# Gate products of the second and third block divided in column blocks and placed between the units of the attentions

## What is computed

```python
# second block: h is the block's input after its first layer norm, 256 x 1024
proj = h @ w_in                                   # 2208 columns: c_q 384, c_kv 256, k_rope 32, q_d, k_d, v_d
q  = rms_norm(c_q)  @ w_q_b                       # 8 heads of 96, MLA
kv = rms_norm(c_kv) @ w_kv_b                      # 8 heads of 64 + 64
o_mla, o_diff = causal attention of q, kv; differential attention of q_d, k_d, v_d with a bias by distance
gates = sigmoid(h @ w_gate + b_gate)              # 2048 columns
mix = (gates[:, :1024] * (o_mla @ w_up_mla) + gates[:, 1024:] * (o_diff @ w_up_diff)) @ w_o
# third block: u is the normed input
qa, ka, va, qb, kb, vb, qi, ki, wi, g = split(u @ w_in)   # 5444 columns, g the last 2048
out_a = attention of qa, ka, va over the 64 best keys by the index scores of qi, ki, wi (DSA)
out_b = causal attention of qb, kb, vb (MoBA, whose one block holds all 256 keys here)
gates = sigmoid(g + b_gate)
h = h + (gates[:, :1024] * (out_a @ w_branch_dsa) + gates[:, 1024:] * (out_b @ w_branch_moba)) @ w_out
```

## Time and profile before

| | |
|---|---|
| time, median of 3 | 2945.77 us |
| profiled execution | 2943.41 us, span 2941.8 us |
| TensorE busy with matmuls | 2766.5 us, 94% |
| VectorE busy | 2075.8 us, 71% |
| ScalarE busy | 1623.6 us, 55% |
| mean granted TensorE clock | 0.957 of full speed |

### The profile page before, as it was taken

One profiled execution on the slowest core, in us unless ns is written; L12 is line 12 of the kernel. 1 busy time (PEld: TensorE's weight loads), 2 busy tenths in 40 slices (PEclk: granted clock), 3 DMA queues, 4 the chain that ended last, 5 costly groups with the idle time before them and its releaser, 6 DMA issues.

```text
span 2941.8 us, 38545 instructions
## 1 busy us (share of the span) xinstructions
PE 2766.5 (94%) x12256; PEld 2192.8 (75%) x12256; DVE 2075.8 (71%) x2462; ACT 1623.6 (55%) x2026; POOL 208.1 (7%) x212
## 2 busy tenths in 40 slices
PE   8997999999999999999799897799997999988999
PEld 5665888888888888888588785677786887876787
DVE  4556999999999999999744664665546445775544
ACT  2323888888888888888544334343443443343443
POOL 0001111111111111111100000000000000100000
PEclk9997999999999999999799997799998999977999
DMA  8755999999999999999755561253554555622564
GB/s 319 233 173 204 357 355 354 355 353 354 358 354 352 355 355 354 355 350 349 255 165 178 168 193 43 82 200 112 170 187 151 178 178 177 185 71 92 169 185 139
DMA packets 263618, 700.16 MB, mean 238 GB/s; under 512 B 29656, under 2 KB 128384, under 8 KB 213824
## 3 DMA queue, kind: packets, MB, share of 16 engines
q1 hardware_dynamic: 249780, 685.13, 66.3%
q0 software_dynamic: 9648, 8.42, 0.9%
q10 hardware_dynamic: 4124, 5.77, 0.6%
HBM read 706.51 MB, written 24.15 MB: 248 GB/s over the span
## 4 chain that ended last, share of the span: by engine, by line
PE 86%; DVE 7%; issue 2%; ACT 2%; DMA 2%; SPq 1%; POOL 0%; DVEq 0%; ACTq 0%; POOLq 0%
PE bank L571 23%; PE bank L572 23%; PE bank L573 23%; PE bank L1025 3%; PE bank L1027 3%; PE bank L1026 3%; PE bank L731 2%; PE bank L689 1%; DMA raw<-in_w_in 1%; PE bank L911 1%; PE bank L707 1%; PE bank L881 1%; PE bank L937 1%; PE bank L637 1%; DVE w_lo L1150 1%
## 5 line engine op out<-in xcount | busy, mean ns | idle before, releaser
L571 PE MATMUL bank<-w_hi,HTh 128*128 128x512 f32 x2964 | 1193.8, 403 | 37.8 <-DVE HTl L1199 33.1
L572 PE MATMUL bank<-w_lo,HTh 128*128 128x512 f32 x2964 | 1177.4, 397 | 0.0
L573 PE MATMUL bank<-w_hi,HTl 128*128 128x512 f32 x2964 | 1177.2, 397 | 0.0
L2058 ACT ACTIVATE w_hi<-raw 128x1024 fp32r<-128x1024 f32 x444 | 461.5, 1054 | 545.8 <-PE bank L573 379.6
L1150 DVE TENSOR_TENSOR w_lo<-raw,w_hi 128x1024 fp32r<-128x1024 f32 x444 | 528.4, 1215 | 309.9 <-ACT w_hi L2058 305.8
L571 PEld LDWEIGHTS bank<-w_hi,HTh 128*128 128x128 f32 x2964 | 563.1, 190 | 179.9 <-DVE HTl L1199 36.9
L573 PEld LDWEIGHTS bank<-w_hi,HTl 128*128 128x128 f32 x2964 | 562.7, 190 | 133.5
L572 PEld LDWEIGHTS bank<-w_lo,HTh 128*128 128x128 f32 x2964 | 563.4, 190 | 123.2
L1773 DVE TENSOR_TENSOR w_lo<-arena,w_hi 128x1024 fp32r<-128x1024 f32 x256 | 315.9, 1234 | 45.5 <-ACT w_hi L2247 45.5
L1773 DVE TENSOR_TENSOR w_lo<-raw,w_hi 128x1024 fp32r<-128x1024 f32 x256 | 298.8, 1218 | 3.4 <-ACT w_hi L2292 2.0
L2247 ACT ACTIVATE w_hi<-raw 128x1024 fp32r<-128x1024 f32 x252 | 266.8, 1059 | 59.2 <-PE bank L573 59.2
(11 more groups left out here) (304 smaller groups left out, 2256.1 us busy)
## 6 DMA issues: line engine op xcount, KB each, us to landing
raw<-in_moe_w SPq DMA_DIRECT2D x128, 1024.0 KB, 4.9
arena<-in_moe_w SPq DMA_DIRECT2D x128, 1024.0 KB, 4.9
raw<-in_ffn_w SPq DMA_DIRECT2D x264, 256.0 KB, 3.4
H<-in_moe_w SPq DMA_DIRECT2D x64, 1024.0 KB, 4.9
MIX<-in_moe_w SPq DMA_DIRECT2D x64, 1024.0 KB, 4.9
raw<-in_ffn_w_gu SPq DMA_DIRECT2D x176, 256.0 KB, 3.4
raw<-in_w_in SPq DMA_DIRECT2D x80, 512.0 KB, 4.7
raw<-in_ffn_w_down SPq DMA_DIRECT2D x88, 256.0 KB, 3.4
```

Of the source, the lines that this page charges most:

```text
L571: pe.matmul(acc, xh, wh, start=start, stop=False)
L572: pe.matmul(acc, xh, wl, start=False, stop=False)
L573: return pe.matmul(acc, xl, wh, start=False, stop=stop)
L2058: act.activation(w_hi[:, n % PARTS, 0:m], raw[:, n % RAW, 0:m], ACT.Copy).then_inc(hi_done, 1)
```

## The change

The gate product of the second block is divided in three: its first 512 columns (`gate2_0`) stand before `q_b`, the next 512 (`gate2_1`) between `kv_b` and the turning of the queries, the last 1024 (`gate2_fill`, 2 blocks) inside the attentions, one block in `A_MLA` and one in `A_DIFF`. The third block's `in3` loses its last 2048 columns; they become `gate3`, 4 blocks, two in `A_MOBA` and two in `A_DSA`. Inside an attention TensorE runs a quantum (`part_of_product`: one 128-deep step for both token tiles, 6 matmuls of 128x512) in each of the first 8 steps, one per step in the second block, two in the third. The blocks use banks 2 and 3 alone, so the scores use 0 and 1. VectorE splits and reads out between the units (`gates_between`, `gates3_between`, `fill_out`), ScalarE makes the high parts there (`highs_between`).

Since `HTh`/`HTl` now have to keep the block's input rows until the end of `A_DIFF`, the latent rows are split into `CTh`/`CTl`, which lie over the bias table and `AFTl`; the bias table of `A_DIFF` is therefore loaded after `kv_b` and not at the end of the first block. The two sigmoids are taken after the second attention of each block, in two halves.

```diff
+FILL_BANK = 2
+QUANTA = 8
-        plan_product("gate2", product(I["w_gate_2"][0], D, 2 * D))
+        plan_product("gate2_0", product(I["w_gate_2"][0][:, 0:512], D, 512))
         plan_product("q_b", ...)
         plan_product("kv_b", ...)
+        plan_product("gate2_1", product(I["w_gate_2"][0][:, 512:1024], D, 512))
+        order.append(("bias2", None))
+        plan_product("gate2_fill", product(I["w_gate_2"][0][:, 1024:2048], D, D))
...
-        plan_product("in3", product(I["w_in_3"][0], D, IN3))
+        plan_product("in3", product(I["w_in_3"][0][:, 0:IN3_QKV], D, IN3_QKV))
+        plan_product("gate3", product(I["w_in_3"][0][:, IN3_QKV:IN3], D, 2 * D))
...
+        CTh = [BIASR[:, k, :] for k in range(5)]
+        CTl = [BIASR[:, 5 + k, :] for k in range(3)] + [AFTl[:, k, :] for k in range(2)]
 # TensorE, in attend
+                def part_of_product():
+                    b, k = blocks[quantum[0] // QUANTA], quantum[0] % QUANTA
+                    t = b.tiles[k // 2]
+                    if k == 0:
+                        pe.wait_ge(fill_read, TT * filled[0])
+                        filled[0] += 1
+                    if k % 2 == 0:
+                        pe.wait_ge(lo_done, t.n + 1)
+                    for tt in range(TT):
+                        mm = three(bank[FILL_BANK + tt][:, :], HTh[:, k, c], HTl[:, k, c], *parts(t.n, k % 2, 512), k == 0, k == KD - 1)
+                    if k % 2 == 1:
+                        mm.then_inc(tile_used, 1)
+                    quantum[0] += 1
                 for i in range(n + LOOKAHEAD + 1):
...
                         values(i - LOOKAHEAD - 1)
+                    if i < n:
+                        for _ in range(each):
+                            part_of_product()
 # TensorE, second block
-            gemm("gate2")
             pe.wait_ge(E("c_norm"), 1)
-            turn_split([PROJ2[:, tt, P * k:P * (k + 1)] for k in range(5) for tt in range(TT)])
-            gemm("q_b")
-            gemm("kv_b", kt0=3)
+            turn_split([PROJ2[:, tt, P * k:P * (k + 1)] for k in range(2) for tt in range(TT)], False)
+            turn_split([PROJ2[:, tt, 2 * P:3 * P] for tt in range(TT)], False)
+            gemm("gate2_0")
+            pe.wait_ge(rows_read, rows[0])
+            gemm("q_b", xh=CTh, xl=CTl)
+            turn_split([PROJ2[:, tt, P * k:P * (k + 1)] for k in (3, 4) for tt in range(TT)])
+            gemm("kv_b", kt0=3, xh=CTh, xl=CTl)
+            gemm("gate2_1")
...
-            attend(A_MLA)
+            attend(A_MLA, blocks=G["gate2_fill"][0:1], each=1)
-            attend(A_DIFF)
+            attend(A_DIFF, blocks=G["gate2_fill"][1:2], each=1)
...
-            attend(A_MOBA)
-            attend(A_DSA)
+            attend(A_MOBA, blocks=G["gate3"][0:2], each=2)
+            attend(A_DSA, blocks=G["gate3"][2:4], each=2)
 # VectorE
+            def fill_out(b, put):
+                dve.wait_ge(tile_used, b.tiles[-1].n + 1)
+                for tt in range(TT):
+                    put(bank[FILL_BANK + tt][:, :], tt, b).then_inc(fill_read, 1)
...
+            def gates_between(b, nxt):
+                def between(i):
+                    if i in (3, 5, 7, 9):
+                        split_to(nxt + (i - 1) // 2)
+                    if i == 8:
+                        fill_out(b, lambda s, tt, b: gate(s, tt, b, D))
+            split_to(first_tile("gate2_fill") + PARTS)
...
+                    if 2 <= i <= 9:
+                        split_to(g3[8 * half + i + 2] + 1)
+                    if i in (4, 8):
+                        fill_out(G["gate3"][2 * half + i // 4 - 1], gate3)
...
 # ScalarE
+                def between(i):
+                    if i in (2, 4, 6, 8):
+                        split_to(nxt + i // 2)
...
+                    if 1 <= i <= 9:
+                        split_to(g3[8 * half + min(i, 8) + 3] + 1)
```

## The result

The changed kernel takes 2907.32 us, the median of 4 runs (2904.60 to 2912.73), where the kernel before, timed beside it, takes 2945.47 (2943.06 to 2946.81): 0.9874 of its time, 95% interval 0.9857 to 0.9891, 38 us less. A second timing beside other kernels gave 2908.59 against 2943.59. The forecast was 2899, with a range from 2883 to 2926. The profiled execution took 2906.68 us against the 2943.41 of before: 36.7 less, where my sum had 49.5, or 46.5 with its allowance for the clock.

What follows compares the result with a forecast made beforehand. TensorE was taken to bound the kernel, with holes and a low clock in the attentions. Second block -26.0 and third -23.5 make -49.5, with 3 for the clock -46.5: from 2943.4 to 2896.9, forecast 2899 us, range 2883 to 2926.

Steps and rivals of the forecast that it cites:

- allowance for the clock: 3 us taken for low clock from waits ahead of the attentions, between 0 and 6; changes -49.5 to -46.5.
- other rivals: ScalarE/VectorE delay third-block units, +14, chance 0.13; bias load delays filling, +7, 0.06; low clock in all attentions, 2994 us, 0.04.
- Steps 1 to 3: Second block: two gate blocks leave the gate product, -22.4 us; shorter waits at latent rows, -5.7, and queries, -2.2.
- Steps 4 and 5: Second block's attentions with filling: `A_MLA` 27.5 us against 24.8, +2.7; `A_DIFF` 31.0 against 27.4, +3.6.
- The first rival: TensorE's clock swings in the second block, whose filling per unit is less than the first block's: +19 us, 2918; chance 0.13.
- Steps 6 and 10: After the second and third blocks' attentions: low parts made earlier, -2 and -2.5 us, the latter with faster row start.
- Step 7: Third block: four gate blocks leave `in3`, -44.8 us; the index columns' copies follow its end, +0.9.
- Step 8: `A_MOBA` becomes VectorE's, with added low parts, readings and a hand-over of 3.4 us: 48.9 against 33.0, +15.9.
- Step 9: `A_DSA`: quanta, a hand-over and last low parts added, some work inside the bias load's wait: 43.9 us against 37.0, +7.

Runs made afterwards that it cites:

- e6_tails: `e1_read_first` with the second bank readings moved to the ninth step's head in all four attentions and the last low parts of DIFF and DSA left until afterwards: 2901.25 us.
- e7_moba_keys_first: The changed kernel with TensorE turning MoBA's queries and keys before the index's behind `in3`: 2908.28 us, beside 2908.59 for the changed kernel.
- e1_read_first: The changed kernel with VectorE reading the first bank pair at the head of the fifth step in MoBA and DSA, not its end: 2897.73 us, again 2900.24.
- e9_busy_wait: The changed kernel with useless TensorE matmuls put into the waits at the two hand-overs, 12 in MoBA and 8 in DSA: 2904.61 us.

## Why the prediction was right, and where it was not

The time lies within the range, 8 us above the forecast; the mechanism held, and sizes were off by place. The granted clock is 0.93 or more in all four attentions, as forecast. Of the other rivals' signs none shows: TensorE waits nowhere for a load of filling tiles, and apart from the two hand-overs at most 1.34 us inside the third block's attentions.

By place, from mark to mark in the two profiles, the second block gave 24.3 us for 26.0 and the third 13.1 for 23.5. The third block's part is made up of: up to the first MoBA score 41.6 us won for 43.9; MoBA 16.0 lost for 15.9; DSA up to the turn behind it 12.9 lost for 7; the stretch up to `out3` 0.4 won for 2.5. So of the 10 us that went missing there, 6 went in DSA, 2 in the index stage and 2 in the stretch behind.

- *Steps 1 to 3, right in the waits.* The latent rows and the queries came out with waits of 0.83, 2.61, 1.48 and 4.26 us against the 0.8, 2.4 and 4.2 priced; the first MLA score comes 28.8 us earlier after the block's first product (30.3 priced). What is missing is the clock: behind the waits of 2.61 and 4.26 us it was 0.74 for 6.5 us and 0.76 for 7.1 us, by my estimate from these two rows 1.7 us each. Behind the 1.48 us it was 1.00.
- *Steps 4 and 5, right.* MLA took 27.53 for 27.5. DIFF is 29.3 at 1.00, and with the wait behind it, up to the turn, it takes 39.7 us against 36.0 before: +3.7 for +3.6. The first rival (a clock that swings in the second block, 2918) did not come: 1.4 us of filling per unit is enough here. The case that the prediction took from the Trainium skill (TensorE: Matmul & The Clock Gate, A second HAM failure mode: psum-queue depth-cycling) did not arise in these two attentions: their clock is 1.00. Whether it was the turnings as such that held the clock down before, as the prediction argues, or the holes that the filling closed, no run tells apart.
- *Steps 6 and 10, wrong.* I gave 2 and 2.5 us for low parts made early. From the turn behind the attention to the start of `o2` it is 31.57 us (1850.43 to 1882.00), before 31.02; to the start of `out3` 31.02, before 31.46. `e6_tails`, which puts the last of those low parts back behind the attentions (one in DIFF, two in DSA), loses nothing there: 30.70 and 30.15. No run shows TensorE waiting for them.
- *Step 7, right*: the turnings behind `in3` begin 44.1 us earlier, for 43.9. But the stage behind it went to a clock of 0.72, 2.4 us that no term had. With shorter waits ahead of it (1.48 us in the kernel before, 1.07 in `e7_moba_keys_first`) the stage keeps 1.00; `e7_moba_keys_first` also shows that VectorE would hold the stage anyway.
- *Step 8, right in sum, wrong in parts.* 48.6 for 48.9. The hand-over was priced 3.4, and moving the reading won 6.8 in `e1_read_first`: I had counted VectorE's own delay, 5.26 us of TensorE's wait are longer than that, and the clock behind was not in it. All the rest was 3.7 cheaper than I had it, probably because low parts and readings fell into holes that I thought filled; no run shows that. So the sum came out by luck.
- *Step 9, the term that failed.* I had 43.9 for DSA, +7 (the terms named there add up to 43.5). It took 50.4 from the first score to the turn, +12.9. The overlap with the bias load was wrong: the first four quanta and two scores I put inside the load's 5.5 us, though by my own prices they are 7.2, and with the clock at 0.69 in the first 5.5 us they took 9.2 (2596.50 to 2605.70), 3.7 more. The load was not what it had been either. VectorE's first soften of DSA (2605.08) starts 8.6 us behind DSA's first score, where it was 6.0 before: ScalarE's queue issues the load 2.2 us behind that score instead of 0.5, since VectorE's reading and low parts now stand ahead of MoBA's last `put`, and the load takes 6.3 us to land instead of 5.4. The third score needs the bank that this soften reads, so at full clock alone most of the 3.7 us would not have come back. Another 1.5 is the clock behind the hand-over, as `e9_busy_wait` shows. The last 1.3 us, behind the bias load and in the last steps, I have not taken apart.
- *The allowance of 3 us for the clock* was meant for waits ahead of an attention. In the third block alone the clock took 2.4 (index stage), 2.4 and 1.5 (the two hand-overs) and some 1.6 us (the start of DSA, 4.54 us for twelve filling matmuls that take 2.97 at full clock), about 8 us in all, each time behind a wait of 1.3 to 5.3 us; the last 1.6 fall together with the wait for the bias load. With the 3.4 us of the second block that is 11 where the sum had 3.

## What to carry to other kernels

Work moved into another stage's holes pays in full only while the engine that gets it does not stand because of it. Price each new wait twice, once for itself and once for the clock behind it: here the second price was between nothing (behind 1.48 us) and 2.4 us (behind 2.11 and 5.26 us), and the length of the wait alone did not tell which. Where two parts of a filling share a bank pair, let the reader free it at the head of its step, ahead of everything that nobody waits for. Gains of one or two us at a seam can be taken back by the clock a few products later, and the same kernel can differ by 2 us in one attention from one execution to another, so read the granted clock of the products behind before you believe a local gain, or its absence.

## What the runs showed of the hardware

- Useless matmuls put into a wait raised the granted clock of the stretch behind it from 0.50 and 0.62 to 1.00, and the kernel got no slower for 20 matmuls more.
- The length of a wait alone did not settle the clock behind it: 1.34 us in DSA's start had 0.69 behind it, 1.48 us had 1.00 in two places (the third group of latent rows, and the index stage of the kernel before), and 2.6 and 2.8 us had 1.00 in one kernel and 0.94 and 0.88 in another with the same matmuls behind them. The two products cost 3.5 us more there.
- 12 matmuls of 128x512 behind a wait: 5.42 us to the next scores at the low level, 3.00 at the high one.
